# Hybrid encoder trunk: triangular inverses whose level of 32x32 blocks multiplies its two corners alone

## What is computed

```python
def step(state, inp):                       # RWKV-7, one token
    rt, wt, kt, at, bt, vt = inp
    sa = jnp.einsum('zbhvk,zbhk->zbhv', state, at)
    state = state * wt[..., None, :] + sa[..., None] * bt[..., None, :] + vt[..., None] * kt[..., None, :]
    return state, jnp.einsum('zbhvk,zbhk->zbhv', state, rt)
...
lhs = jnp.where(strict, jnp.einsum('zbhnid,zbhnjd->zbhnij', kb, k) * decay, 0.0) + jnp.eye(C)   # gated DeltaNet
u_base = lax.linalg.triangular_solve(lhs, v * beta[..., None], left_side=True, lower=True, unit_diagonal=True)
k_cum = lax.linalg.triangular_solve(lhs, kb * jnp.exp(gc)[..., None], left_side=True, lower=True, unit_diagonal=True)
```

## Time and profile before

| | |
|---|---|
| three executions | 1645.86, 1646.08, 1649.13 us |
| the profiled execution's own time | 1646.1 us |
| span from its first to its last instruction | 1644.0 us |
| TensorE busy | 1622.3 us, 99% |
| VectorE, ScalarE, GpSimd busy | 1229.5, 980.7 and 108.5 us |
| mean granted TensorE clock | 0.994 |
| inverses and outputs of passes 0 to 3 | about 155 to 248 us |
| inverses of passes 4 and 5 | about 588 to 622 us |
| experts | from about 660 us |

### The profile page before, as it was taken

One profiled execution on the slowest core, in us unless ns is written; L12 is line 12 of the kernel. 1 busy time (PEld: TensorE's weight loads), 2 busy tenths in 40 slices (PEclk: granted clock), 3 DMA queues, 4 the chain that ended last, 5 costly groups with the idle time before them and its releaser, 6 DMA issues.

```text
span 1644.0 us, 21942 instructions
## 1 busy us (share of the span) xinstructions
PE 1622.3 (99%) x8450; PEld 1223.6 (74%) x8450; DVE 1229.5 (75%) x1222; ACT 980.7 (60%) x956; POOL 108.5 (7%) x111
## 2 busy tenths in 40 slices
PE   8999999999999999999999999999999999999997
PEld 4868996999988875777677677677677777777775
DVE  6578555645523773788988988888888888888886
ACT  3356334433443432677777777777777777777774
POOL 2005120000000020000000100100100100100000
PEclk9999999999999999899999999999999999999999
DMA  7311014556443211899999999999999999999993
GB/s 251 109 52 52 1 52 154 175 185 205 148 167 122 103 52 53 337 412 412 367 391 361 370 386 361 371 386 362 371 380 367 373 382 359 378 381 363 412 372 138
DMA packets 101892, 438.56 MB, mean 267 GB/s; under 512 B 11114, under 2 KB 34942, under 8 KB 58814
## 3 DMA queue, kind: packets, MB, share of 16 engines
q1 hardware_dynamic: 99102, 427.90, 68.7%
q0 software_dynamic: 2720, 9.70, 2.0%
HBM read 430.62 MB, written 6.95 MB: 266 GB/s over the span
## 4 chain that ended last, share of the span: by engine, by line
PE 95%; DVE 2%; ACT 2%; DMA 0%; issue 0%; SPq 0%; ACTq 0%; DVEq 0%
PE bank L2937 18%; PE bank L2939 18%; PE bank L2938 18%; PE bank L2709 5%; PE bank L2633 4%; PE bank L2634 4%; PE bank L2632 4%; PE bank L2195 3%; PE bank L2872 2%; PE bank L2159 2%; PE bank L2584 2%; PE bank L2378 1%; PE bank L2403 1%; PE bank L2996 1%; DVE split L2088 1%; PE bank L2173 1%
## 5 line engine op out<-in xcount | busy, mean ns | idle before, releaser
L2088 DVE TENSOR_TENSOR split<-ring,split 128x2048 fp32r<-128x2048 f32 x336 | 762.0, 2288 | 119.2 <-ACT split L1236 116.1
L1236 ACT ACTIVATE split<-ring 128x2048 fp32r<-128x2048 f32 x336 | 641.7, 1916 | 168.9 <-PE bank L2939 168.3
L2937 PE MATMUL bank<-split 128*96 128x512 f32 x896 | 354.4, 396 | 1.4 <-DVE split L2049 0.7
L2939 PE MATMUL bank<-split 128*96 128x512 f32 x896 | 351.2, 392 | 0.0
L2938 PE MATMUL bank<-split 128*96 128x512 f32 x896 | 351.1, 392 | 0.0
L2937 PEld LDWEIGHTS bank<-split 128*96 128x96 f32 x896 | 144.7, 161 | 62.3 <-DVE split L2088 3.7
L2939 PEld LDWEIGHTS bank<-split 128*96 128x96 f32 x896 | 144.6, 161 | 61.5
L2938 PEld LDWEIGHTS bank<-split 128*96 128x96 f32 x896 | 144.7, 162 | 57.6
L2937 PE MATMUL bank<-split,ehr_ 128*96 128x512 f32 x448 | 177.5, 396 | 2.1 <-DVE split L2088 2.0
L2939 PE MATMUL bank<-split,ehr_ 128*96 128x512 f32 x448 | 175.6, 392 | 0.0
L2938 PE MATMUL bank<-split,ehr_ 128*96 128x512 f32 x448 | 175.5, 392 | 0.0
(11 more groups left out here) (538 smaller groups left out, 1886.8 us busy)
## 6 DMA issues: line engine op xcount, KB each, us to landing
ring<-in_od_moe_gate SPq DMA_DIRECT2D x112, 1024.0 KB, 7.2
ring<-in_od_moe_up SPq DMA_DIRECT2D x112, 1024.0 KB, 7.5
ring<-in_od_moe_down SPq DMA_DIRECT2D x112, 1024.0 KB, 7.2
ring<-in_od_w_in SPq DMA_DIRECT2D x7, 2048.0 KB, 7.8
ring<-in_ev_ffn_gate SPq DMA_DIRECT2D x11, 1024.0 KB, 5.4
ring<-in_ev_ffn_up SPq DMA_DIRECT2D x11, 1024.0 KB, 8.0
ring<-in_ev_w_in SPq DMA_DIRECT2D x5, 2048.0 KB, 8.9
ring<-in_ev_ffn_down SPq DMA_DIRECT2D x5, 2048.0 KB, 7.8
```

The lines of the kernel that those rows point to most:

```text
L1236: act.activation(wst[:, r % NSTAGE, 0, :], ring[:, (r % NHALF) * HALF:(r % NHALF + 1) * HALF], ACT.Copy).then_inc(w_hi, 1)
L2088: dve.tensor_tensor(wst[:, r % NSTAGE, 1, :], ring[:, (r % NHALF) * HALF:(r % NHALF + 1) * HALF], wst[:, r % NSTAGE, 0, :].bitcast(F32), S ...
L2937: pe.matmul(o, hi, wh, start=start, stop=False)
L2939: return pe.matmul(o, lo, wh, start=False, stop=stop)
```

## The change

At level 5 (blocks of 32) the two corners between paired blocks, rows 0 to 31 against 32 to 63 and rows 64 to 95 against 96 to 127, are multiplied alone, as products of 32x32 (`QUARTERS`, `quarter`). They are read straight from A, so GpSimd makes a mask for level 4 only. A call of TensorE has 8 such products in place of 4 of 128 columns, the corners in turn for each matrix u. The two results of one u lie in the same bank, on partitions 0 to 31 and 64 to 95, 32 columns apart. The transposes of level 5 take the first 96 rows and columns, ScalarE copies from them the even blocks alone, and VectorE copies the two corners into P, which holds nothing there yet, in place of the sum. Levels 4 and 6 stay as they are.

```diff
--- before.py
+++ after.py
@@ -454,17 +454,22 @@
             return (p * (NLEV - LEV0) + lev - LEV0) * 2 + g + 1
 
         def mask_seq(p, lev, g):
-            return (p * (NLEV - 1 - LEV0) + lev - LEV0) * 2 + g + 1
-
-        def off_diagonal(p, g):
-
-            return (Atile[p] if p < 4 else Ao[:, p - 4])[64:128, 4 * g:4 * g + 4, 0:64]
+            return (p * (NLEV - 2 - LEV0) + lev - LEV0) * 2 + g + 1
+
+        def off_diagonal(p, g, rows_, cols_):
+
+            return (Atile[p] if p < 4 else Ao[:, p - 4])[rows_, 4 * g:4 * g + 4, cols_]
 
         def corner(bank, r, at=0):
 
             return bank[r, :].rearrange("p (u w) -> p u w", u=4)[:, :, at:at + 64]
 
+        def quarter(bank, r, at):
+
+            return bank[r, :].rearrange("p (u w) -> p u w", u=4)[:, :, at:at + 32]
+
         LOW, HIGH = slice(0, 64), slice(64, 128)
+        QUARTERS = [(slice(64 * t, 64 * t + 32), slice(64 * t + 32, 64 * t + 64)) for t in range(2)]
 
         def turn_seq(p, lev, g):
             return (sum(NLEV - 1 - LEV0 for q in range(p)) + lev - 1 - LEV0) * 2 + g + 1
@@ -682,18 +687,16 @@
             def level_masks(p, mats, blocks):
 
                 Am = INVB[p][3]
-                for lev in range(LEV0, NLEV - 1):
+                for lev in range(LEV0, NLEV - 2):
                     for g in range(2):
-                        if lev > LEV0:
-                            pool.wait_ge(x_ps, inv_seq(p, lev - 1, g))
-                        elif p == 0:
+                        if p == 0:
                             pool.wait_ge(vt_sb, 2)
                             pool.wait_ge(q_rdy, 4)
                             pool.wait_ge(dve_step, DVE_STEPS["bon_cp"])
                         elif p == 4:
                             pool.wait_ge(dve_step, DVE_STEPS[blocks])
                         else:
-                            pool.wait_ge(x_ps, inv_seq(p - 1, NLEV - 2, g))
+                            pool.wait_ge(x_ps, inv_seq(p - 1, NLEV - 3, g))
                         m = levmask[:, lev - LEV0, :].unsqueeze(1).to_broadcast([P, 4, P])
                         pool.tensor_tensor(Am[g], mats[g], m, MUL).then_inc(am_rdy, 1)
 
@@ -953,6 +956,10 @@
                             act.wait_ge(tt_ps, turn_seq(p, lev, g))
                         if lev == NLEV - 1 and INV[p][g][0] == 0:
                             act.activation(INVB[p][0][g][LOW, :, LOW], corner(B[2 + g], LOW), ACT.Copy).then_inc(t_cp, 1)
+                        elif lev == NLEV - 2:
+                            bank = B[2 + g][:, :].rearrange("p (u s) -> p u s", u=4)
+                            act.activation(odd_even(INVB[p][0][g], lev, False)[0:96], odd_even(bank, lev, False)[0:96],
+                                           ACT.Copy).then_inc(t_cp, 1)
                         elif lev > LEV0:
                             act.activation(INVB[p][0][g], B[2 + g][:, :].rearrange("p (u s) -> p u s", u=4),
                                            ACT.Copy).then_inc(t_cp, 1)
@@ -1559,7 +1566,10 @@
                 Tm, Pm = INVB[p][0], INVB[p][1]
                 for g in range(2):
                     dve.wait_ge(pt_ps, inv_seq(p, lev, g))
-                    if lev < NLEV - 1:
+                    if lev == NLEV - 2:
+                        for t, (e, o) in enumerate(QUARTERS):
+                            last = dve.tensor_copy(Pm[g][e, :, o], quarter(B[2 + g], e, 32 * t))
+                    elif lev < NLEV - 1:
                         pv = odd_even(Pm[g], lev, True)
                         last = dve.tensor_tensor(pv, packed(B[2 + g], lev, 0), pv, ADD)
                     elif INV[p][g][0] == 0:
@@ -2362,7 +2372,7 @@
                     pe.wait_ge(tp_sb, n - 2)
                 if lev == NLEV - 1:
                     for u in range(4):
-                        last = pe.matmul(corner(B[g], LOW)[:, u, :], off_diagonal(p, g)[:, u, :], Pm[g][HIGH, u, HIGH],
+                        last = pe.matmul(corner(B[g], LOW)[:, u, :], off_diagonal(p, g, HIGH, LOW)[:, u, :], Pm[g][HIGH, u, HIGH],
                                          start=True, stop=True)
                     last.then_inc(x_ps, 1)
                     for u in range(4):
@@ -2372,15 +2382,21 @@
                             last = pe.transpose(B[2 + g][:, P * u:P * u + P], Pm[g][:, u, :], ident[:, :])
                     last.then_inc(tt_ps, 1)
                     return
+                if lev == NLEV - 2:
+                    for u in range(4):
+                        for t, (e, o) in enumerate(QUARTERS):
+                            last = pe.matmul(quarter(B[g], e, 32 * t)[:, u, :], off_diagonal(p, g, o, e)[:, u, :],
+                                             Pm[g][o, u, o], start=True, stop=True)
+                    last.then_inc(x_ps, 1)
+                    for u in range(4):
+                        last = pe.transpose(B[2 + g][0:96, P * u:P * u + 96], Pm[g][0:96, u, 0:96], ident[0:96, 0:96])
+                    last.then_inc(tt_ps, 1)
+                    return
                 pe.wait_ge(am_rdy, mask_seq(p, lev, g))
                 pm = odd_even(Pm[g], lev, True)
                 for u in range(4):
                     last = pe.matmul(packed(B[g], lev, 0)[:, u], Am[g][:, u, :], pm[:, u], start=True, stop=True)
                 last.then_inc(x_ps, 1)
-                if lev > LEV0:
-                    for u in range(4):
-                        last = pe.transpose(B[2 + g][:, P * u:P * u + P], Pm[g][:, u, :], ident[:, :])
-                    last.then_inc(tt_ps, 1)
 
             def level_pt(p, lev, g):
 
@@ -2393,7 +2409,11 @@
                 pe.wait_ge(x_cp, inv_seq(p, lev, g))
                 xm = odd_even(Xm[g], lev, True)
                 for u in range(4):
-                    if end and z == 1:
+                    if lev == NLEV - 2:
+                        for t, (e, o) in enumerate(QUARTERS):
+                            last = pe.matmul(quarter(B[2 + g], e, 32 * t)[:, u, :], Tm[g][e, u, e], Xm[g][e, u, o],
+                                             start=True, stop=True)
+                    elif end and z == 1:
                         last = pe.matmul(corner(B[2 + g], HIGH, 64)[:, u, :], Xm[g][LOW, u, HIGH], Tm[g][LOW, u, LOW],
                                          start=True, stop=True)
                     elif end:
```

## The result

The changed kernel takes **1670.26 us** (median of 4 runs, 1661.46 to 1679.22) against 1645.97 us (4 runs, 1645.1 to 1649.13): a ratio of 1.0151, 95% interval 1.0123 to 1.0179. It is slower by 24.3 us where 1636.4 was forecast. A ratio in this text counts only the runs within 1.5% of the fastest of their kernel, which leaves out three of e8_fill128's ten runs, two of e11_two128's seven and two of e14_between's twelve, so these three ratios look better than the medians beside them.

The account below looks back on a forecast made before the run. TensorE, busy 99% of the span, was taken as the bound, the order of its own instructions setting the pace. Six passes at 1.62 us less gave 9.7 us off 1646.1, so 1636.4 us, range 1634.0 to 1643.5.

Parts of the forecast that it names:

- A call of 16 records in 0.25 us: TensorE, level 5: 16 records of 32 columns, two corners side by side, take 0.25 us where 8 wide ones took 0.89.
- floor: Rival: a record costs near 0.058 us however few its columns, a call 0.93, total time 1649.8 us; chance 0.10.
- in turns: Rival: level 5's two corners take turns on TensorE, a call 0.50 us, total time 1640.9 us; chance 0.20.
- drain: Rival: every change of corner at level 5 drains the array, a call 1.7 us, total time 1668 us; chance 0.06.
- Steps to another shape 0.09 and 0.15, transposes 0.34: TensorE, level 5: shape changes cost 0.09 us into products, 0.15 into transposes; transposes of 96 columns 0.34 after 0.44.
- VectorE's pair 0.58: VectorE, level 5: two copies of 128 elements replace one sum of 256 (0.42 us) and take 0.58, bounds 0.52 to 0.83.
- The two short waits: TensorE waits briefly for ScalarE's copy of T before the second product, and for VectorE before level 6.
- GpSimd is worth nothing: GpSimd: dropping 12 of its 24 mask products gains nothing, since they were hidden behind level 4.
- 1.62 us a pass less: First pass: level 6 starts at 164.93 in place of 166.55, so level 5 is 1.62 us shorter.
- 6 x 1.62 = 9.7 us: All six passes gain the same 1.62 us, taking 9.7 us off the total time.
- A microsecond taken from the chain here should shorten the run by one: TensorE in the inverses: later loads wait for buffers TensorE or its followers free, so chain savings pass fully to the total.
- If a stretch behind takes the gain back: Sign that the prediction is wrong: a later stretch loses what level 5 gained; the other such sign was a call over 0.6 us.

Follow-up runs that it names:

- e8_fill128: Changed kernel plus one unread 128x128 product of 128 moving columns a pass, between level 5's two products with T: 1662.22 us, ratio 1.0085.
- e11_two128: Changed kernel plus two unread products of 128 moving columns a pass, one after each product with T of level 5: 1642.84 us, ratio 0.9968.
- e14_between: Changed kernel plus one unread product of 256 moving columns a pass, ahead of level 6's first product: 1653.04 us, ratio 1.0026.
- e9_small: Changed kernel plus 32 unread 32x32 products (64 records) a pass between level 5's two products with T: 1649.02 us, ratio 1.0013.
- e4_half: Changed kernel with two 64x64 halves, 32 moving columns each, in place of 32x32 for X and product with T at level 5: 1670.75 us, ratio 1.0155.
- e3_full: Changed kernel with TensorE's level 5 work back at 128x128, GpSimd's masks still gone and VectorE's and ScalarE's copies kept: 1645.06 us, ratio 0.9995.
- e1_fill1: Changed kernel plus one unread 128x128 product of 512 moving columns a pass, between level 5's two products with T: 1641.00 us, ratio 0.9979.
- e2_fill2: Changed kernel plus two unread products of 512 moving columns a pass, one after each product with T of level 5: 1644.95 us, ratio 1.0009.
- e5_xonly: Changed kernel with 32x32 corners kept in level 5's X only, product with T back at 128x128: 1640.72 us, ratio 0.9975.
- e7_fill256: Changed kernel plus one unread product of 256 moving columns a pass, between level 5's two products with T: 1638.54 us, ratio 0.9962.
- e10_before_fill: Kernel before the change plus one unread product of 256 moving columns a pass, between level 5's two products with T: 1648.47 us, ratio 1.0014.
- e12_best: Same kernel as e7_fill256, in five more runs: 1637.57 us, ratio 0.9946 to the kernel before.
- e15_pt_between: Changed kernel with level 5's X back at 128x128, plus one unread product of 256 moving columns a pass ahead of level 6: 1642.65 us, ratio 0.9993.
- e13_first: Changed kernel plus one unread product of 256 moving columns a pass, ahead of level 5's first X: 1678.89 us, ratio 1.0212.

## Why the prediction was wrong

Step by step, by its own parts:

- **A call of 16 records in 0.25 us: right.** Product plus the step to the transposes is 0.37 (159.87 to 160.24), forecast 0.40. With the step at 0.15 the call is 0.22, or 0.028 for a record in each of the two corners. The step of 0.15 is the forecast's, but e9_small bears the price out without it: 96 such records from 161.09 to 162.54, 0.015 each. No run times one corner alone, so that the two run side by side is shown for the 64x64 halves of e4_half (0.055 a pair, one alone 0.058) and only likely for the corners. Both corners, and both halves in e4_half, write one bank, in other partitions. The rule that the prediction weighed (the Trainium skill, "TensorEngine Tiling (Array Packing)", section "Restrictions and Gotchas": other row tiles cannot access one bank at the same time) would give 0.50; the trace doesn't agree with it, at least for other partitions of the bank. The floor of the Trainium skill's "TensorE: Matmul & The Clock Gate", section "Back-to-back issue gap", about 62 ns a MATMUL where the sequencer decodes, would by the prediction's estimate have made 0.99 of the call; the trace has 0.22, so no such floor binds here. The rivals in turns, floor and drain all fall with the 0.37. The prediction's "where one alone costs 0.11" isn't in those rows; the 0.11 is that of 128 weight columns in the earlier trace rows.
- **Steps to another shape 0.09 and 0.15, transposes 0.34: right.** Transposes to the next product 0.46 (160.24 to 160.70), forecast 0.43.
- **VectorE's pair 0.58: right** (four copies in 1.19 us, 284 ns each), and so is what it starts on. ScalarE's copy of the turned matrix takes 0.38:

```profile
160.81 0.38 ACT L961 ACTIVATE arena<-bank 96x256 f32<-96x256 f32 x1
...
162.03 1.19 DVE L1571 COPY arena<-bank 32x128 f32<-32x128 f32 x4 [0.43 <-PE bank L2414]
```

- **The two short waits: right.** The product with T waits for ScalarE 6 times, 1.3 us in all, and level 6 for VectorE's copies 6 times, 1.5 us in all.
- **GpSimd is worth nothing: right** (e3_full, ratio 0.9995). It has 12 masks left and nobody waits for it.
- **1.62 us a pass less: right**, 1.71 by the rows (4.50 less 2.79), of which the forecast gave 0.09 to the step ahead of the first product. With the clock held this is also what the end gets: e1_fill1, e2_fill2, e3_full, e5_xonly, e7_fill256, e10_before_fill, e12_best and e15_pt_between (chain 4.05, 1643.3) lie within 1.4 us of 1646.0 less 6 x what the chain lost.
- **The step that failed is the one from there to the sum**: "6 x 1.62 = 9.7 us" prices every other product of the run at its old duration, with the clock at 1.00. It is the prediction's "A microsecond taken from the chain here should shorten the run by one", and it held only where the clock was held. In place of 9.7 us gained, work at the lower clock cost about 40. The prediction read this clock as a property of the stretch, and it is a result of what TensorE does in it. The change took most of the product work out of level 5, ahead of a level 6 that was sparse already, and the clock fell just behind, for the products with 128 weight columns that make up most of a pass. No rival named this, and no term was put for it. The range's upper end of 1643.5 left it out altogether.
- "If a stretch behind takes the gain back" was named as what would prove the prediction wrong, but without a mechanism, a price or a chance. That is where it went.
- The rival of a drain at each corner change gave 1668 us, near what was measured. It is wrong all the same: a call takes 0.22 us, not 1.7. A time that fits doesn't show a mechanism.

What the experiments show: the whole loss is clock (span times clock is the same in the four runs, and the clock's rows give 39.8 us from 150 to 300 us alone); the cause lies in TensorE's instructions of level 5, not in the other engines (e3_full); it needs neither the 32x32 shape (e4_half) nor the waits (e8_fill128), and the steps between shapes don't bring it about (e1_fill1); one wide product in the right place undoes it (e12_best); and its place counts (e13_first). What stays open: why unread 32x32 products undo two thirds of it (e9_small), how much of a filler's effect is its work and how much the wait that it fills, and what exactly the chip weighs when it takes the clock back; e14_between shows that it decides differently from run to run.

A hint was there and I read past it: the kernel itself issues unread products in another stage (the helper `unread(n)`, L2906 of the changed kernel). Work that nobody reads, on the engine that is the bound, asks for a reason.

## What to carry to other kernels

A cut of product work on a TensorE that is the bound is priced twice: once by the time of the instructions that go, and once by the clock at which those that stay will run, so a forecast of smaller products needs a rival in which the granted clock behind them falls. "Busy 99%" doesn't protect: look at the granted clock by stretches of 25 us and at the records per stretch, since busy time is the same at either level. Where small products stand in a row, try one unread wide product in the middle of them, and test its place: here ahead of them it didn't hold the clock, and behind them it held the clock only in some executions. In the middle, 0.6 us a pass turned 1.5% slower into 0.4 to 0.5% faster.

## What the runs showed of the hardware that was not expected

- TensorE's clock fell to the 1.2 GHz level while the engine was busy 24.5 of 25 us, with no wait longer than 0.3 us in the stretch; before it fell, TensorE had done the 32x32 products, the 96x96 transposes and the 64x64 products of levels 5 and 6, and products with 128 weight columns before those. The fall itself lies within the products that begin at 164.55.
- Variants between two outcomes vary from run to run: e8_fill128 from 1642.5 to 1672.8 us, e14_between from 1638.1 to 1675.1, each with the mean clock to match. A single run of such a kernel tells little, and e8_fill128's profiled one, at 1642.52, was its fastest.
- A record in each of two 32x32 corners, in other rows and other columns of the array and into other partitions of one bank, cost 0.028 us together, weight loads included (0.22 over 8, with the step taken as 0.15; 0.030 by e9_small's 96 records in 1.45 us). In e4_half a record in each of two 64x64 halves cost 0.055 (0.59 less the step of 0.15, over 8), and one of 64x64 alone takes 0.058 (with 64 moving columns, where the pairs have 32), so the pairs run side by side there; a corner alone was not timed.
- Small products in a wait kept much of the clock: e9_small, with 64 unread records of 32x32 a pass, took 1649.02 us where the changed kernel took 1670.26.
- An fp32 product with 128 weight columns and 512 moving ones takes 1.05 us with its steps (163.27 to 164.32 in e1_fill1), one of 256 columns 0.63 (164.36 to 164.99 in e12_best), one of 128 columns 0.42 (164.18 to 164.60 in e8_fill128).
